# Gate matrices of a PEER layer as three bfloat16 products of one-hots, on one NeuronCore

## The reference

```python
sc, ci = lax.top_k(cand, PEER_TOPK)
eid = (jnp.take_along_axis(i1, ci // PEER_TOPK, -1) * N_KEYS
       + jnp.take_along_axis(i2, ci % PEER_TOPK, -1))
gate = jax.nn.softmax(sc, -1)
hid = jax.nn.gelu(jnp.einsum('td,thkd->thk', xt, expert_u[eid], ...))
return jnp.einsum('thk,thkd->td', (gate * hid).astype(xt.dtype), expert_v[eid])
```

## Time and profile before

| | |
|---|---|
| median of 3 runs | 2097.69 us (2092.4 to 2098.9) |
| the profiled execution | 2096.14 us, span 2094.4 us |
| busy of the span | PE 96%, PEld 88%, DVE 76%, ACT 38%, POOL 25% |
| mean granted clock of PE | 0.982 of full speed |

### The profile page before, as it was taken

How to read it: one execution, slowest core, us unless ns; L and a number is a source line. 1 busy time by engine, 2 the same in 40 slices (tenths; PEclk the granted TensorE clock), 3 DMA queues, 4 the chain that set the end, 5 groups by cost and what they waited for, 6 DMA issues and landing times. The chain is left out here.

```text
span 2094.4 us, 33809 instructions
## 1 busy us (share of the span) xinstructions
PE 2012.4 (96%) x12943; PEld 1845.7 (88%) x12943; DVE 1596.5 (76%) x2880; ACT 793.5 (38%) x1311; POOL 514.9 (25%) x334
## 2 busy tenths in 40 slices
PE   8999879889999899999999999999999999999998
PEld 8998879778866899999999999999988888888886
DVE  6635766565254467999997698888869999999997
ACT  4335454442341322232244444444444333333332
POOL 0000020000000000122224422222328655656630
PEclk9999989989999999999999999999999999999999
DMA  5233210061451403688888978888899999999982
GB/s 173 82 101 117 81 53 1 32 216 41 178 192 56 127 36 109 223 292 282 284 278 306 347 245 264 262 269 265 266 342 411 411 411 411 411 411 409 405 349 93
DMA packets 205519, 483.74 MB, mean 231 GB/s; under 512 B 11983, under 2 KB 104655, under 8 KB 205286
## 3 DMA queue, kind: packets, MB, share of 16 engines
q1 hardware_dynamic: 159334, 314.56, 41.6%
q0 software_dynamic: 46080, 167.79, 22.4%
HBM read 423.29 MB, written 58.36 MB: 230 GB/s over the span
## 5 line engine op out<-in xcount | busy, mean ns | idle before, releaser
L3024 PE MATMUL ps<-v_high_low,gated_high_low 128*128 128x512 f32 x2304 | 526.0, 391 | 4.5 <-ACT gated_high_low L3092 4.5
L3024 PEld LDWEIGHTS ps<-v_high_low,gated_high_low 128*128 128x128 f32 x2304 | 434.4, 189 | 96.0 <-ACT v_high_low L3090 4.8
L2641 PE MATMUL ps<-x_high_low,u_high_low 128*128 128x384 f32 x1024 | 355.6, 347 | 0.2 <-ACT u_high_low L2707 0.2
L2642 PE MATMUL ps<-x_high_low,u_high_low 128*128 128x384 f32 x1024 | 345.0, 337 | 0.0
L3116 POOL DMA_INDIRECT outputs<-peer_v,kept x138 | 250.3, 1814 | 169.3 <-DVE kept L3133 125.0
L2758 POOL DMA_INDIRECT scores<-peer_u,kept x64 | 82.0, 1281 | 737.2 <-DVE kept L2870 515.7
L2771 DVE TENSOR_TENSOR u_high_low<-ps,u_high_low 128x1024 fp32r<-128x1024 f32 x128 | 156.4, 1222 | 82.7 <-ACT u_high_low L2707 82.0
L2716 ACT ACTIVATE kept<-ps 128x384 f32<-128x384 f32 x128 | 62.9, 491 | 407.5 <-PE ps L2646 404.3
L2646 PE MATMUL ps<-x_high_low,u_high_low 128*128 128x384 f32 x1024 | 204.8, 342 | 0.0
L2641 PEld LDWEIGHTS ps<-x_high_low,u_high_low 128*128 128x128 f32 x1024 | 192.5, 188 | 0.5 <-ACT u_high_low L2707 0.5
L2642 PEld LDWEIGHTS ps<-x_high_low,u_high_low 128*128 128x128 f32 x1024 | 192.8, 188 | 0.0
(11 more groups left out here) (489 smaller groups left out, 4087.0 us busy)
## 6 DMA issues: line engine op xcount, KB each, us to landing
experts<-peer_u SPq DMA_DIRECT2D x63, 1024.0 KB
raw_v<-peer_v SPq DMA_DIRECT2D x60, 1024.0 KB
hidden<-kept SPq DMA_DIRECT2D x64, 384.0 KB
gates<-scores SPq DMA_DIRECT2D x12, 2048.0 KB, 10.3
first_hidden<-hidden SPq DMA_DIRECT2D x16, 768.0 KB, 9.3
outputs<-gates SPq DMA_DIRECT2D x16, 768.0 KB
outputs<-hidden SPq DMA_DIRECT2D x16, 768.0 KB
first_gates<-gates SPq DMA_DIRECT2D x15, 768.0 KB
```

Of the source, the lines that this page charges most:

```text
L2641: pe.matmul(o, utr[:, b, HI, k], xr[:, HI, k, 0:DN], start=(k == 0), stop=False)
L2642: pe.matmul(o, utr[:, b, HI, k], xr[:, LO, k, 0:DN], start=False, stop=False)
L3024: ins = pe.matmul(bank(c, 2 * t + h), gr[:, slot, x, DN * b + P * t:DN * b + P * t + P], vr[:, slot, y, D * b + 512 * h:D * b + 512 * h + ...
```

## The change

The keys, the one-hots and the gates become bfloat16. The gate is split into three bfloat16 parts whose sum is exact, the gated one-hot becomes three matrices side by side (3072 elements for eight tokens), and PE adds three bfloat16 products per token in PSUM in place of one float32 product. The first one-hot now has a buffer of its own, `hot1`. In `pick` the slot numbers `places` and the row of numbers they are compared with (`iota16`) become bfloat16 too, and the written cost of that comparison goes from 4.5 to 2.4. The core of the diff:

```diff
-    kept, kt = words(c, H_K, NT, 3, 128), words(c, H_T, 4, DN)
+    keys_of, raw_gate, pieces = words(c, H_T, DN).bitcast(BF16), words(c, H_T + DN, DN), words(c, H_T + 2 * DN, PIECES_OF * DN // 2).bitcast(BF16)
...
-                    ins = pe.matmul(bank(c, 6 + i % 2)[:, P * t:P * t + P], hot2[slot][:, cols], gated[slot][:, cols], start=True, stop=True)
+                    o, one, parts = bank(c, 6 + i % 2)[:, P * t:P * t + P], hot2[slot][:, first + t], gated[slot][:, first + t]
+                    for j in range(PIECES_OF):
+                        ins = pe.matmul(o, one, parts[:, j], start=(j == 0), stop=(j == PIECES_OF - 1))
...
-                act.copy(kt[:, 0:3, P * n:P * n + P], bank(c, 6 + n % 2, 3 * P).rearrange("p (i t) -> p i t", i=3)).then_inc(pairs_out, 1)
+                act.copy(keys_of[:, :, P * n:P * n + P], bank(c, 6 + n % 2, 2 * P).rearrange("p (i t) -> p i t", i=2)).then_inc(pairs_out, 1)
+                act.copy(raw_gate[:, P * n:P * n + P], bank(c, 6 + n % 2)[:, 2 * P:3 * P]).then_inc(pairs_out, 1)
...
-                step(v.tensor_tensor(spots, over(places[:, :, 0:hp], 3, [P, 2, hp, 16]), over(over(iota[:, 0:16], 1, [P, hp, 16]), 1, [P, 2, hp, 16]),
+                step(v.tensor_tensor(spots, over(places[:, :, 0:hp], 3, [P, 2, hp, 16]), over(over(iota16[:, 0:16], 1, [P, hp, 16]), 1, [P, 2, hp, 16]),
                                      ALU.is_equal))
-                paced(4.5 * part)
+                paced(2.4 * part)
...
+            step(v.tensor_copy(iota16, iota))
...
-            v.tensor_tensor(kt[:, 3], gate, inv, ALU.mult).then_inc(gates_set, 1)
+            step(v.tensor_tensor(full, gate, inv, ALU.mult))
+            step(v.tensor_copy(pieces[:, 0], full))
+            step(v.tensor_tensor(left, full, pieces[:, 0], ALU.subtract))
+            step(v.tensor_copy(pieces[:, 1], left))
+            v.tensor_tensor(pieces[:, 2], left, pieces[:, 1], ALU.subtract).then_inc(gates_set, 1)
...
+                keys = over(iota16, 1, [P, OCT, NK])
+                after(v, hot_set, o)
+                v.tensor_tensor(hot1, keys, over(keys_of[:, 0, t0:t0 + OCT], 2, [P, OCT, NK]), ALU.is_equal).then_inc(hot_first, 1)
+                v.tensor_tensor(hot2[slot], keys, over(keys_of[:, 1, t0:t0 + OCT], 2, [P, OCT, NK]), ALU.is_equal)
                 v.wait_ge(hot_first, o + 1)
-                v.tensor_tensor(k1, k1, over(kt[:, 3, t0:t0 + OCT], 2, [P, OCT, NK]), ALU.mult).then_inc(hot_set, 1)
+                v.tensor_tensor(gated[slot], over(hot1, 2, [P, OCT, PIECES_OF, NK]),
+                                over(pieces[:, :, t0:t0 + OCT].rearrange("p i t -> p t i"), 3, [P, OCT, PIECES_OF, NK]), ALU.mult).then_inc(hot_set, 1)
```

More of the change, by code:

```diff
@@ L2451 @@
 P_HID = P_IDS + ROWSETS
-assert H_RX + D == EARLY_AT[0] and EARLY_AT[0] + 512 <= P_IDS
+PIECES_OF = 3
+assert H_RX + D == EARLY_AT[0] and EARLY_AT[0] + 512 + NK // 2 <= P_IDS
+assert 2 * DN + PIECES_OF * DN // 2 <= 4 * DN and 4 * DN + OCT * P // 2 <= PH * 256 and 2 * PIECES_OF * OCT * P // 2 <= 2 * 3 * 4 * P
 F_GST = (F_SC, F_SC + NK * TG)
@@ L2523, in phase_hidden @@
     rows = (row[0], row[1].bitcast(U32), row[2].bitcast(U32), row[3].bitcast(U32), row[4], row[5], tail, second)
-    places = words(c, H_B + 512, 2, PAIRS)
-    kept, kt = words(c, H_K, NT, 3, 128), words(c, H_T, 4, DN)
+    places = row[1].bitcast(BF16).rearrange("p (s r) -> p s r", s=2)
+    kept = words(c, H_K, NT, 3, 128)
+    keys_of, raw_gate, pieces = words(c, H_T, DN).bitcast(BF16), words(c, H_T + DN, DN), words(c, H_T + 2 * DN, PIECES_OF * DN // 2).bitcast(BF16)
+    keys_of, pieces = keys_of.rearrange("p (i t) -> p i t", i=2), pieces.rearrange("p (i t) -> p i t", i=PIECES_OF)
     gate, inv = words(c, H_V, DN), words(c, H_V + DN, DN)
-    firm = plain(c.hot[:, :])
-    hot2, gated = [firm[:, 0:OCT * P], firm[:, 2 * OCT * P:3 * OCT * P]], [firm[:, OCT * P:2 * OCT * P], words(c, H_HOT, OCT * P)]
+    full, left = raw_gate, inv
+    hot1 = words(c, H_T + 4 * DN, OCT * P // 2).bitcast(BF16).rearrange("p (t k) -> p t k", t=OCT)
+    hot2 = [words(c, H_HOT + OCT * P // 2 * i, OCT * P // 2).bitcast(BF16).rearrange("p (t k) -> p t k", t=OCT) for i in range(2)]
+    gated = [x.bitcast(BF16).rearrange("p (t i k) -> p t i k", t=OCT, i=PIECES_OF) for x in (
+        c.hot[:, PIECES_OF * OCT * P // 2 * i:PIECES_OF * OCT * P // 2 * (i + 1)] for i in range(2))]
+    iota16 = words(c, EARLY_AT[0] + 512, NK // 2).bitcast(BF16)
     gst = [words(c, a, NK, TG) for a in F_GST]
@@ L2684, in _ @@
                 if n >= 2:
-                    pe.wait_ge(pairs_out, n - 1)
+                    pe.wait_ge(pairs_out, 2 * (n - 1))
                 for i in range(3):
@@ L2740, in _ @@
                 act.wait_ge(pairs_turned, n + 1)
-                act.copy(kt[:, 0:3, P * n:P * n + P], bank(c, 6 + n % 2, 3 * P).rearrange("p (i t) -> p i t", i=3)).then_inc(pairs_out, 1)
-            act.wait_ge(pairs_out, DENSE)
-            act.activation(gate, kt[:, 2], ACT.Exp).then_inc(exps, 1)
+                act.copy(keys_of[:, :, P * n:P * n + P], bank(c, 6 + n % 2, 2 * P).rearrange("p (i t) -> p i t", i=2)).then_inc(pairs_out, 1)
+                act.copy(raw_gate[:, P * n:P * n + P], bank(c, 6 + n % 2)[:, 2 * P:3 * P]).then_inc(pairs_out, 1)
+            act.wait_ge(pairs_out, 2 * DENSE)
+            act.activation(gate, raw_gate, ACT.Exp).then_inc(exps, 1)
             both(BEFORE - 1, 0)
@@ L2828, in pick @@
                 paced(0.8)
-                v.tensor_tensor(hif, hif, tail, ALU.add)
-                step(v.tensor_tensor(lof, lof, second, ALU.add))
+                v.tensor_tensor(places[:, 0, 0:hp], hif, tail, ALU.add)
+                step(v.tensor_tensor(places[:, 1, 0:hp], lof, second, ALU.add))
                 paced(0.8)
                 spots = hot16[:, 0:2 * hp * 16].rearrange("p (s r j) -> p s r j", s=2, j=16)
-                step(v.tensor_tensor(spots, over(places[:, :, 0:hp], 3, [P, 2, hp, 16]), over(over(iota[:, 0:16], 1, [P, hp, 16]), 1, [P, 2, hp, 16]),
+                step(v.tensor_tensor(spots, over(places[:, :, 0:hp], 3, [P, 2, hp, 16]), over(over(iota16[:, 0:16], 1, [P, hp, 16]), 1, [P, 2, hp, 16]),
                                      ALU.is_equal))
-                paced(4.5 * part)
+                paced(2.4 * part)
                 for i in range(2):
```

5 lines of the change are left out of this document (removed).

## The result

The changed kernel takes 2150.47 us (median of 4 runs, 2147.7 to 2155.48), the kernel before 2097.86 (4 runs) beside it: the ratio is 1.0266, with a 95% interval of 1.0253 to 1.0279. It is slower by 2.7%; the forecast was 2153. The profiled execution took 2147.79 us, 51.7 more than the 2096.14 of before.

The account below looks back on a forecast made before the run. PE sets the octet stage's pace before the change, DVE after it: 55.0 (steps) + 2.5 (opening) + 2.13 - 2.2 (end) = +57.4 us on the profiled 2096.1, 2153.5, stated as 2153. Range 2126 to 2172 us.

Parts of the forecast that it names:

- DVE becomes the bound: Octet stage: DVE's step grows from 5.93 to 7.99 us, over PE's 6.82; +55.0 us over 47 steps; chance 0.78.
- The third operation at +2.13 us: DVE's gating per octet grows from 1024 to 3072 elements: 2048 more at 1.04 ns each.
- the 5.93 us of work: DVE's work per octet step before the change: the 6.82 us step less 0.89 us of waits for ACT.
- The reason, a repeated element: DVE's octet operations repeat an element innermost, so 16-bit types stay at 1.04 ns an element; L2834 and L2846 as grounds.
- PE's product at 105 ns: Each of 24 bfloat16 products per unit costs 105 ns, between bounds of 58 and 119; hidden behind DVE.
- PE's unit: PE's octet-stage unit, 6.82 us less 1.90 for two old calls plus 24 products: 7.44 us, low bound 6.31, high 7.78.
- the break-even: Product price at which PE's unit stays as long as before: 1.90 / 24 = 79 ns.
- Rival 1: Octet stage: DVE quick and products 58 to 75 ns, so PE's unit shrinks; about 2074 to 2093 us; chance 0.09.
- The opening: Before octet 0: two DVE subtractions and two casts, about 1.9 us, plus 0.6 for ACT's split copies; 2.5 us later.
- The end: Last octet: PE takes it at once at 1596.1 us, where before it took it at 1538.66; shift 57.5 us.
- The picks at 0: Picks, 812 to 1115 us: DVE's cover shrinks from 11 to about 3 us; cost 0, up to 5 if it fails.
- rival 4: Octet stage: DVE slow and PE's clock falls because PE waits each unit; 2194 us at clock 0.84; chance 0.05.

Follow-up runs that it names:

- Experiment 2: Changed kernel with PE making one product per token in place of three, DVE still making all three parts: 2151.78 us, ratio 1.0263 to the kernel before.
- experiment 3: Changed kernel with DVE gating one part (1024 elements) in place of three, PE multiplying that part three times: 2082.9 us, ratio 0.9936 to the kernel before.
- experiment 8: Changed kernel with the picks as before (slot numbers float32, written cost 4.5), octets still changed: 2152.03 us, ratio 1.0272 to the kernel before.
- turned: Experiment 1: changed kernel with eight tokens innermost in one-hots and gated matrices, PE's columns 16 bytes apart: 2311.37 us, ratio 1.1024 to the kernel before.
- experiment 4: Changed kernel plus single DVE operations on unused memory behind the last pick, to read their durations: one execution, 2168.07 us including them.
- pairs: Experiment 5: changed kernel with two tokens innermost, columns 4 bytes apart, gating as three operations of 1024 elements: 2083.68 us, ratio 0.9946 to the kernel before.
- quads: The kernel with two tokens innermost, changed to four, so weights and moving columns lie 8 bytes apart: one execution, 2154.24 us.
- weights_pitch: Changed kernel with only the second one-hot, PE's weights, laid out 16 bytes between columns, moving operand unchanged: one execution, 2129.4 us.

## Why the prediction was right

**DVE becomes the bound: right.** Experiment 2 takes two thirds of PE's products away and nothing changes; experiment 3 takes the third operation's growth away and the loss is gone.

**The third operation at +2.13 us: right.** It takes 3353 ns, 2131 more than a one-hot. Predicted was a step of 7.99 us, measured 7.915. The 2.13 is exact, and so are the 0.07 of the `dot`s (experiment 8), so the difference lies in the 5.93 us of work that was worked out as step less waits; that term was 1% too large, 3.7 us over the stage. The rows show why: when DVE has no wait, the next operation starts 0.08 us before the last one's record ends (in the unit above `low` starts 3.27 us after the gating, whose record is 3.35). Ahead of a wait that overlap is missing, and step less waits counts it as work. Without the 39 waits it comes back: 3.1 of the 3.7 us.

**The reason, a repeated element: right, but one of its grounds was not.** Experiments 1 and 4 show it with the same elements and types. As the prediction quotes it, "Vector Engine (DVE) Microarchitecture Reference" in the Trainium skill (Performance modes) says the same of one element read again and again, and the traces agree (1225 ns against 691). The tier table by type, also quoted there, would have had the gating at about 1.75 us; measured 3.35. But L2846 doesn't show what the prediction read from it. It has no repeated element; gaps around runs of two explain a part of its time (618 of 758 ns), and a repeated pair costs nothing (693).

**PE's product at 105 ns: wrong, and hidden.** It costs 56 ns, about half, and a little less than the lower bound of 58. The 105 came from products of 64 columns with float32 weights; from them the prediction read that the weight load sets the price, and with bfloat16 weights a load and a product together stay at 56. Of the two figures that it quotes for such a product, 56 ns is met, with a weight load each, and 81 ns is not.

**PE's unit: a second error, hidden as well.** The prediction took 1.90 us off for the old calls, the time between starts of weight loads; on PE's own starts they took 1.70 (experiment 3). So the unit of its lower bound, 6.31 us, was too short although the product's price was nearly right, and the break-even is 1.70 / 24 = 71 ns, not 79. Had DVE kept the double rate with no cost on PE, the step would have been PE's 6.5 us and the time near 2083, where experiments 3 and 5 stand. Rival 1 had 2074 to 2093 for that case, and holds it although the product was cheaper than its 58 to 75 ns, because the two errors go against each other. The size that the prediction called decisive only "if DVE is quick" is the one it had worst.

**The opening: 1.7 us against 2.5.** DVE's part was right (two subtractions at 0.56, casts at 0.36, 1.98 us with the gaps); its inverse began 0.25 us earlier than before, at 1207.74. ACT's split of its copies was put down as +0.6 and didn't delay DVE: the exponential ends at 1203.4, long before DVE reaches the inverse at 1207.7.

**The end: 53.0 against 57.5 us of shift** for PE's last first call: 0.8 of the opening, 3.7 of the steps. **The picks at 0: right** (experiment 8). **The clock (rival 4): did not matter.** It was 1.00 in 1300 to 1400 (0.99 from 1215 to 1590), and at 0.93 in experiment 2 the time still stood.

**A slip in the sum.** 2153.5 is the working's time for the profiled execution, and the median was said to be 1.6 higher, so the forecast by that working is 2155, not 2153. The sum itself, +57.4 us on the profiled execution, met +51.7; that 2153 lies only 2.5 us from the measured median owes 2 us to the slip.

## What to carry to other kernels

Before a change gives an engine more elements of a narrower type, look at the innermost axis of every operand: on DVE one repeated element costs the double rate, a repeated pair doesn't, so interleave two of whatever is repeated. The same layout is read by PE, and there the distance between moving columns has its own price: a stride of two 16-bit elements is nearly free (57 ns against 56), a stride of four doubles a product's cost, so pick the smallest interleave that the other engine needs. And find the slack of the engine that gets more work first (here DVE's 0.89 us of waits per step): with DVE at its slow rate it told that the change had to lose, without knowing PE's price. And price an engine's work by the starts of one engine throughout: weight loads and matmuls gave 1.90 and 1.70 us for the same two calls.

## What the runs showed of the hardware

The price of one bfloat16 product of 128 columns, with a weight load each, by the distance between columns. It is the time of a unit's two calls on PE, from the first product to the start of the matmul behind, over 24:

| moving columns | weights' columns | ns each | kernel |
|---|---|---|---|
| 2 bytes | 2 bytes | 56 | after |
| 4 bytes | 4 bytes | 57 | pairs |
| 8 bytes | 8 bytes | 113 | quads |
| 16 bytes | 16 bytes | 229 | turned |
| 2 bytes | 16 bytes | 65 | weights_pitch |

From 4 bytes on the price doubles with the distance, and the last row leaves little of that to the weights. In the Trainium skill "SBUF — State Buffer" (Door 1: The DMA port swizzle, the note on cachelines) says that consecutive accesses run at full bandwidth as long as at least two fall in one line of 16 bytes, and that bfloat16 can be strided by 8 elements for free. At 8 bytes, a stride of 4, two do, and the product costs twice as much; at 16 bytes, a stride of 8, it costs four times as much. So the runs don't bear it out for PE's moving operand. The 4-byte row fits any such rule.

Going from float32 matmuls to bfloat16 products cost PE nothing that shows: the first product starts 0.18 us after the last 384-column matmul, as a float32 product did. Only the weight load loses its lead of 0.17 us, and PEld shows 0.16 us of "issue" for it.

The clock fell in `turned` although PE's record has no gap. By the prices PE's unit would be 5.17 + 5.49 = 10.66 us, and most units take 10.80 (1300.10 to 1310.90), but 13 of the 47 are about 1.5 us longer, every third or fourth. In these the granted clock falls to its lower level, 1.2 GHz, while PE runs the float32 matmuls behind the second call. The windows are the stage, 10.8 us at full clock without a gap on PE, and a slow stretch right behind; then two matmuls of that stretch:

```profile
1215.00:1735.00 520.00, 518.39 (x2585) 413.53 (x2584) 251.13 (x291) 158.41 (x185) 59.35 (x50) 0.95 0.51 164
...
1250.00:1260.80 10.80, 10.80 (x58) 8.52 (x57) 5.24 (x6) 3.43 (x4) 1.15 (x1) 1.00 0.28 95
...
1262.10:1265.00 2.90, 2.90 (x11) 2.90 (x11) 1.56 (x2) 1.07 (x2) 0.00 (x0) 0.52 0.52 147
...
1263.06 0.52 PE L2651 MATMUL ps<-x_high_low,u_high_low 128*128 128x384 f32 x1
1263.38 0.52 PE L2650 MATMUL ps<-x_high_low,u_high_low 128*128 128x384 f32 x1
```

There 384-column matmuls start 0.32 us apart in place of 0.17. Over the stage that is about 20 us. In pairs, whose PE is as busy (272.65 of the 275 us from 1215 to 1490), the clock was 1.00. What in `turned` lowers it is not shown.
